# A single-core transformer pair on Trainium2: another order of two norms, of the compression steps and of the linear attention

## The reference

```python
# end of block 1: x = x + z @ w_down, then its final norm
x = x + (jnp.square(jax.nn.relu(h2 @ w_up)) @ w_down)
x = rmsnorm(x, final_norm_g)
# block 2, on h = rms_norm(x, ln_mix_g) @ w_in_2, split into its parts:
k_cmp = gelu(flat_k @ cmp_w1_k) @ cmp_w2_k      # compression, 15 blocks per head
v_cmp = gelu(flat_v @ cmp_w1_v) @ cmp_w2_v
o_nsa = gated sum of attention over k_cmp, over blocks, over a window   # 8 heads
o_gla = rms_norm(gated linear attention, chunks of 64 tokens) * silu(r) # 4 heads
x = x + (merge(o_nsa, o_gla) @ w_out_2)
# then cross attention to a memory of 256 tokens, and a gated feed-forward block
```

## Time and profile before

| what | us |
| --- | --- |
| runs: lowest, median, highest | 845.38, 846.78, 848.41 |
| the profiled execution, its own time | 845.38 |
| its span in the profile | 843.5 |
| busy: PE, DVE, ACT, POOL | 820.2, 598.5, 455.0, 95.4 |
| the chain that ended last, on PE | 86% of the span |

### The profile page before, as it was taken

One profiled execution on the slowest core, in us unless ns is written; L12 is line 12 of the kernel. 1 busy time (PEld: TensorE's weight loads), 2 busy tenths in 40 slices (PEclk: granted clock), 3 DMA queues, 4 the chain that ended last, 5 costly groups with the idle time before them and its releaser, 6 DMA issues.

```text
span 843.5 us, 13091 instructions
## 1 busy us (share of the span) xinstructions
PE 820.2 (97%) x5359; PEld 731.6 (87%) x5359; DVE 598.5 (71%) x945; ACT 455.0 (54%) x798; POOL 95.4 (11%) x106
## 2 busy tenths in 40 slices
PE   6999999999999999999999999999998999999997
PEld 4878887779999888889998699999886999999885
DVE  5878766877666745567568766856768699899644
ACT  5756556545554634454575555652578455554433
POOL 4110000000000000000400000000000455555100
PEclk9999999999999999999999999999999999999999
DMA  8844644455655455464864433335543465564551
GB/s 292 249 163 150 201 136 152 163 162 183 221 194 190 170 192 197 150 223 144 241 212 152 134 94 110 101 100 176 201 148 100 151 200 171 180 200 167 190 193 50
DMA packets 85387, 143.47 MB, mean 170 GB/s; under 512 B 5026, under 2 KB 43200, under 8 KB 85328
## 3 DMA queue, kind: packets, MB, share of 16 engines
q1 hardware_dynamic: 83008, 137.11, 49.5%
q0 software_dynamic: 2160, 5.46, 2.2%
q10 hardware_dynamic: 160, 0.07, 0.0%
HBM read 141.05 MB, written 1.05 MB: 168 GB/s over the span
## 4 chain that ended last, share of the span: by engine, by line
PE 86%; DVE 8%; ACT 4%; DMA 1%; issue 1%; SPq 0%; DVEq 0%; ACTq 0%
PE PS L1221 83%; PE PS L1230 2%; DVE low_r L2246 2%; DMA low_f<-in_w_in_dram 1%; ACT WK_f L1759 1%; DVE AR_f L2254 1%; ACT high L1762 1%; DVE AR_f L2246 1%; DVE X L2246 1%; DVE HTl_r L2246 0%; ACT AR_f L1756 0%; ACT HTh L1762 0%; DVE WK_f L2254 0%; DVE WK_f L2250 0%; DVE HTl_f L2246 0%
## 5 line engine op out<-in xcount | busy, mean ns | idle before, releaser
L2246 DVE TENSOR_TENSOR low_r<-low_f,high 128x1024 fp32r<-128x1024 f32 x254 | 324.6, 1322 | 85.5 <-ACT high L1762 85.2
L1762 ACT ACTIVATE high<-low_f 128x1024 fp32r<-128x1024 f32 (+1 forms) x262 | 257.0, 1030 | 73.8 <-DMA low_f<-in_w_down_dram 34.5
L1221 PE MATMUL PS<-HTh,high 128*128 128x256 f32 x888 | 253.7, 286 | 2.1 <-DVE HTl_r L2246 1.1
L1221 PE MATMUL PS<-HTl_r,high 128*128 128x256 f32 x888 | 251.2, 283 | 0.0
L1221 PE MATMUL PS<-HTh,low_r 128*128 128x256 f32 x856 | 242.1, 283 | 0.0
L1221 PE MATMUL PS<-high,AR_r 128*128 128x512 f32 (+1 forms) x656 | 193.3, 376 | 1.0 <-DVE AR_f L2254 1.0
L1221 PEld LDWEIGHTS PS<-HTh,high 128*128 128x128 f32 x888 | 169.6, 191 | 3.9 <-issue 2.3
L1221 PEld LDWEIGHTS PS<-HTl_r,high 128*128 128x128 f32 x888 | 169.7, 191 | 0.1
L1221 PEld LDWEIGHTS PS<-HTh,low_r 128*128 128x128 f32 x856 | 163.5, 191 | 0.0
L1221 PEld LDWEIGHTS PS<-high,AR_r 128*128 128x128 f32 (+1 forms) x656 | 116.6, 180 | 25.3 <-DVE AR_f L2254 1.2
L1221 PE MATMUL PS<-low_r,AR_r 128*128 128x512 f32 (+1 forms) x328 | 121.1, 373 | 0.0
(11 more groups left out here) (183 smaller groups left out, 850.9 us busy)
## 6 DMA issues: line engine op xcount, KB each, us to landing
low_f<-in_w_in_dram SPq DMA_DIRECT2D x40, 1024.0 KB, 5.2
low_f<-in_w_up_dram SPq DMA_DIRECT2D x38, 1024.0 KB, 5.2
low_f<-in_w_down_dram SPq DMA_DIRECT2D x27, 1024.0 KB, 4.9
low_f<-in_w_out_dram SPq DMA_DIRECT2D x8, 1024.0 KB, 5.1
low_f<-in_w_xkv_dram SPq DMA_DIRECT2D x4, 1024.0 KB, 5.4
low_f<-in_w_branch_gla_dram SPq DMA_DIRECT2D x2, 1024.0 KB, 5.2
low_f<-in_w_branch_nsa_dram SPq DMA_DIRECT2D x2, 1024.0 KB, 5.1
low_f<-in_w_xq_dram SPq DMA_DIRECT2D x2, 1024.0 KB, 5.1
```

Of the source, the lines that this page charges most:

```text
L1221: return nc.tensor.matmul(o, l, r, start=start, stop=stop, skip_group_check=True)
L1762: return nc.scalar.activation(o, i, ACT.Copy, bias=0.0, scale=1.0)
L2246: return nc.vector.tensor_tensor(o, a, b, op)
```

## The change

Six edits to the order; no instruction is added, dropped or resized.
- TWO_NORMS has 20 characters instead of 18. The first three pieces of norm 0 no longer come before the first piece of M: the sums of block 0 come after one piece, `two_gained` after two, `scaled` after six. The sums of block 1 come after five pieces instead of four. The transposes of block 0 come before the last half of `kx`.
- `rows` no longer calls `lows` after its last piece.
- `cmp_z` c=1 moves behind `cmp_g` c=0, and the `lows` ahead of that `cmp_g` goes. One yield less stands between `cmp_t` and `cmp_o`.
- `cmp_m` writes banks 0 and 1 (`gbank`) instead of 4 and 5. Bank 0 is also that of `gla_a`, the step before.
- `gla_m` moves from `nsa` (after `nsa_e` 0) to the start of `gla`, with a yield of its own, and three yields go from the rest of `gla`.
- With one yield less before `nsa`, each piece of fill stands one piece later relative to the attention steps.

```diff
--- before.py
+++ after.py
@@ -27,7 +27,7 @@
 
 GATE_ORDER = (2, 0, 3, 1)
 ATTN_RATIO = (1.0, 2.0)
-TWO_NORMS = "000MMMM1M11MMM0M1M"
+TWO_NORMS = "M0M0MMM1M0M10MM1MM1M"
 
 CONST = {}
 _at = 0
@@ -447,8 +447,6 @@
                 if i == 1:
                     self.done(self.U[key, 1, 1].full if q == 3 else None)
                     self.ahead(end + 2)
-                    if q == 3:
-                        self.lows()
                 yield
 
     def chain(self, *gens):
@@ -636,8 +634,7 @@
         self.small(("gat",))
         self.step("gat")
         next(q)
-        for c in range(2):
-            self.step("cmp_z", c=c)
+        self.step("cmp_z", c=0)
         for br in range(2):
             self.small(("kv", br, 2), True)
             self.step("kv", br=br, part=2, u=u)
@@ -651,8 +648,8 @@
         self.step("gla_c")
         self.cmp_first(0)
         self.step("gla_e")
-        self.lows()
         self.step("cmp_g", c=0)
+        self.step("cmp_z", c=1)
         yield
         yield
         self.cmp_first(1)
@@ -662,7 +659,6 @@
             self.small(("ct", c))
             self.step("cmp_t", c=c)
         yield
-        yield
         for c in range(2):
             self.gbank(("co", c))
             self.step("cmp_o", c=c)
@@ -670,7 +666,7 @@
 
     def cmp_first(self, c):
         u = self.take("w1")
-        self.use(("cm", c), [4 + c])
+        self.gbank(("cm", c))
         self.step("cmp_m", c=c, u=u)
         self.done(self.U["cm", c].full)
 
@@ -678,29 +674,27 @@
         def bank0(key):
             return self.use(key, [0])
 
+        self.step("gla_m")
+        yield
         bank0(("gk",))
         self.step("gla_k")
         yield
-        bank0(("gs", 0))
-        self.step("gla_s", n=0)
-        yield
-        yield from self.gla_scores(0, bank0)
-        for n in range(1, 3):
+        for n in range(3):
             bank0(("gs", n))
             self.step("gla_s", n=n)
             yield
-        yield from self.gla_sums(0, bank0)
+            if n == 0:
+                yield from self.gla_scores(0, bank0)
+            elif n == 2:
+                yield from self.gla_sums(0, bank0)
         self.step("gla_n", i=0)
         yield
-        yield
         yield from self.gla_scores(1, bank0)
-        yield
         yield
         yield from self.gla_sums(1, bank0)
         self.step("gla_n", i=1)
         yield
         self.step("gla_r")
-        yield
         yield
         yield
         for i in range(2):
@@ -742,8 +736,6 @@
                 self.step("nsa_t", n=n - 1)
             if n < 8:
                 self.step("nsa_e", n=n)
-            if n == 0:
-                self.step("gla_m")
             if n > 0:
                 yield
                 self.aux(("no", n - 1))
```

## The result

The changed kernel takes 856.34 us as the median of three runs (856.10 to 857.63), the kernel before 846.78. Over all runs of both on one chip the ratio is 1.0127, 95% interval 1.0094 to 1.0161: 1.3% slower, between 8 and 14 us. The forecast was +7.1 us (853.9). The direction and most places were right, the size was too small: 1.27% of 846.78 is 10.8 us, which is above the upper end of the range (857.3 is +10.5). The three runs by themselves differ by +9.6.

What follows compares the result with a forecast made beforehand. PE was taken as the bound, busy 820.2 of 843.5 us, with in-order ACT and DVE queues behind it. New waits of 3.9 + 3.2 = 7.1 us gave 853.9, 0.8% slower; 8-in-10 range 849.3 to 857.3.

Steps and rivals of the forecast that it cites:

- part one: Reordered norms and missing `lows`: new PE waits of 1.4 us before unit 59 and 2.5 before XN's transposes, +3.9 in sum.
- The thin margin at `kvc`: Low halves of HT ready 0.2 us or more before the `kvc` product; if missed too, the norms' sum becomes 5.
- The bank wait: At `cmp_m` 0, now in bank 0 just written by `gla_a`, PE waits for DVE's reader: +1.9 us.
- `cmp_o`: PE waits for `cmp_t`'s copies, behind splits 72 and 73 on DVE, with one product less between: +0.9 us (0.5 to 1.5).
- `nsa_t` 0: The old PE wait of 0.63 us goes, as `nsa_w` 0 and `nsa_s` 1 no longer stand behind `gla_m`: -0.6.
- `gla_k`: PE waits for `gla_m`, now behind `nsa_w` 0, `nsa_s` 1 and split 75 on DVE: +1.6 us (0.5 to 2.5).
- In the sum it costs nothing: The clock term: the 2.5 us wait at XN's transposes is near the edge for half clock, but counted as 0.
- rival three: Clock falls, the `kvc` margin fails or later pieces lose theirs: +10, 857 us, chance 0.1; half-rate stretch loses 1.9 or so.
- From 490 to 562 ... I take 0: Same steps one fill piece apart; DVE finishes `gla_r` three us before PE asks for it: 0, with 0 to 1.
- part two: Compression and linear attention, 420 to 490 us: seven terms of waits opened and closed, +3.2 us in sum (1 to 5).
- `cmp_m` 1, +0.8: PE waits at `cmp_m` 1 for split 70, now behind `cmp_g` 0 and `cmp_z` 1 on DVE: +0.8 us (0.2 to 1.3).
- The rival on the other side: DVE reaches the moved steps before PE, so gaps close and none open, decided at `gla_m`: -2.8, 844.0 us, chance 0.06.

Runs made afterwards that it cites:

- bank_back: The changed kernel with `cmp_m` writing banks 4 and 5 again: median 856.83 us, ratio 1.0118 to the kernel before.
- norms_only: The kernel before with only the new TWO_NORMS and `rows` without its call of `lows`: median 851.48 us, ratio 1.0060.
- second_only: The changed kernel with the old TWO_NORMS and the call of `lows` in `rows` restored: median 854.42 us, ratio 1.0090 to the kernel before.
- bank_only: The kernel before with one edit, `cmp_m` in banks 0 and 1: median 848.11 us, ratio 1.0016.
- close_four_b: close_three with the low parts of units 73 and 74 moved behind the copies of `cmp_t` and `cmp_o` on DVE: median 843.43 us, ratio 0.9960 to the kernel before.
- close_three: The kernel before with four moves of splits, `nsa_e` 0, `gla_m` and other steps, aimed at its three old waits: median 844.51 us, ratio 0.9971.

## Why the prediction was right or wrong

- **"Nothing to win before 420, only gaps to open": right.** Both waits of part one are where they were put, with the releasers named. ACT and DVE came a little earlier than counted:

```profile
367.86 2.01 ACT L1754 ACTIVATE high<-low_f 128x1024 fp32r<-128x1024 f32 x2 [12.58 <-DMA low_f<-in_w_xkv_dram]
...
371.09 1.99 ACT L1754 ACTIVATE high<-low_f 128x1024 fp32r<-128x1024 f32 x2
372.99 0.61 ACT L1751 ACTIVATE AR_f<-XN 128x512 f32<-128x512 f32 x1
...
374.34 0.21 DVE L2243 TENSOR_SCALAR st<-st 128x1 f32<-128x1 f32 x1 [3.03 <-ACT AR_f L1751]
...
376.25 4.62 DVE L2238 TENSOR_TENSOR low_r<-low_f,high 128x1024 fp32r<-128x1024 f32 x4
380.79 1.28 DVE L2238 TENSOR_TENSOR XN<-X,grow 128x512 f32<-128x512 f32 x2
382.00 0.75 DVE L2242 TENSOR_SCALAR XN<-XN,st 128x1024 f32<-128x1024 f32 x1
```

  This trace runs 0.2 ahead of that of before. The split of unit 58 began at 367.86, the squares of `two_gained` ended at 374.3 (forecast 374.6), the first half of unit 59 at 377.5 (377.9), `scaled` at 382.75 (383.3). Each count came out 0.3 to 0.55 late, 0.2 of it the earlier start of this trace, and so both waits 0.35 too long. "The thin margin at `kvc`" held.
- **The bank wait, `cmp_o`, `nsa_t` 0 and `gla_k`: right to 0.2 us** in the trace. All of these were counted in the same way, by walking DVE's and ACT's queue row by row to the moved step. For `cmp_o` the closeness is partly luck: with the same order its wait was 0.58 to 1.08 over the seven traces that have it, by how late PE came there.
- **The clock: one of the two steps that failed.** "In the sum it costs nothing" was wrong: it cost 1.3 us of path in the first trace of the changed kernel and 5.7 in the second. Over all runs I estimate some 2 us, the 10.8 of the ratio less the 8.7 of the waits. It rested on one wait of 1.57 us with a clock of 1.00 behind it. That was one execution. In the 14 traces of this study the clock fell at or near that same place in ten. It fell behind the wait of 2.1 at XN in four of eight traces, behind the bank wait at `cmp_m` 0 in seven of eight, behind the 1.47 at `nsa_v` 3 in three of five, and behind the 1.65 at `gla_k` in one of five. Each fall before `bn` cost 1.1 to 3.1 us of path (rival three counted 1.9). The spread of the kernel before, 845.38 to 848.41, was the sign that I had and did not use: the waits come out the same in every trace of one order but for some tenths, so most of a difference of 3 us has to come from something that one trace need not show. As a rival (+10, chance 0.1) the mechanism was there with about its right size; as a part of the most likely case it should have had 1 to 3 us.
- **"From 490 to 562 ... I take 0": the other step that failed.** It counted when DVE finishes `gla_r`, and did not ask which banks `gla_t` and `gla_o` share with their new neighbours: 0.76 before `nsa_t` 1 (inside the stretch of part two, and in no term) and 1.47 before `nsa_v` 3. Together 2.2 us of idle time, more than the clock took in the first trace. The terms that the forecast had came out 1.5 us below it in sum (5.6 for 7.1), so the error of the whole is smaller than that of these two steps.
- **`cmp_m` 1, +0.8: covered** by the half clock ahead of it, as bank_back shows.
- **"So what is lost stays lost": right** between part one and part two, by norms_only and second_only; within part two single terms do trade with each other (bank_only 0.7, not 1.89; bank_back no gain).
- **The old waits, "everything the change can win there": right in size.** close_four_b takes exactly these and gets 2.3 of the 2.8; small waits of 0.37 and 0.21 are left.
- The rival on the other side (DVE early at `gla_m`) did not come: DVE was done with it at 470.4, and PE had been done with the product ahead of `gla_k` since 468.8.

## What to carry to other kernels

When a step moves, write down two things for it and not one: when its inputs are ready on the engines that feed it, and which step now writes the same bank right behind it and what stands ahead of the reader of that bank. The dearest wait here (3.62) was for a reader of a bank queued behind 2.35 us of bulk work (a low part). And the 1.01 of close_three, for copies queued behind two low parts, closed when one low part moved behind them. Where PE is full, price every new wait above its own length by what the clock does behind it, and take that price from the spread of many runs, not from a single trace.

## What the runs showed of the hardware

- The granted clock fell to 0.50 behind waits of PE of 1.5 to 3.6 us, and also not behind the same wait of the same kernel in another execution (XN: 1.00 in the first trace of the changed kernel, 0.51 in the second; both waits 2.14 to 2.15). Each stretch at half between unit 58 and `bn` (434.0 to 437.0 above, 467.6 to 474.4 in second_only) cost 1.1 to 3.1 us of path. The Trainium skill, page "TensorE: Matmul & The Clock Gate", section "Why this matters for your kernels", asks that inner gaps between bursts be kept short. The traces agree in the direction, but give no length below which a gap is safe: of equal gaps some had a fall behind them and some had not.
- Which executions have it cannot be read from the order of the work. It shows in the mean clock of an execution: the changed kernel at 854.9 to 855.2 with a mean clock of 0.996, and at 861.4 to 861.7 with 0.987 to 0.989. What sets it off in one execution and not in the next was not tried and stays open.
- A wait costs PE some 0.1 to 0.2 us more than its idle time in the profile, since the product before it and the one after it no longer overlap.
